# The end of attention by token tiles, with six smaller edits, in a kernel of three transformer blocks on one core

## What is computed

```python
h = _rmsnorm(x, mix_norm[l])
c_q, c_kv, k_pe, hq, hf, hi, hg = jnp.split(h @ w_in[l], splits, axis=-1)
a = _mla(c_q, c_kv, k_pe, positions, ...)      # 4 heads, causal softmax attention
r = _hgrn2(hq, hf, hi, hg, lower[l], hg_out_norm[l])
x = x + jnp.concatenate([a, r], axis=-1) @ w_out[l]
x = x + (_swiglu(...) if l == 0 else _moe(...))

# _mla: q = _rmsnorm(c_q) @ w_q_b, kv = _rmsnorm(c_kv) @ w_kv_b, both with rotary parts
s = jnp.where(key_idx <= q_idx, qn @ kn.T + qp @ kp.T, NEG_BIG)
o = jax.nn.softmax(s, axis=-1) @ v

# _hgrn2
f = lb + (1.0 - lb) * jax.nn.sigmoid(z)
log_f = jnp.log(f)
k = (1.0 - lb) * jax.nn.sigmoid(-z)
# per chunk, b = cumsum(log_f): attn = sum_d q k exp(b_t - b_s), plus a state carried on
o = _rmsnorm(o, out_norm) * jax.nn.silu(g)
```

## Time and profile before

| | |
|---|---|
| median of 3 runs | 1884.51 us (1883.92 to 1885.49) |
| the profiled execution | 1884.52 us, of which the span is 1882.6 us |
| PE busy | 1859.7 us, 99% of the span |
| DVE, ACT, POOL busy | 1520.7, 1240.1, 402.8 us |
| TensorE clock granted (PEclk) | 9, that is 90% or more, in all 40 slices |
| PE's share of the chain that ended last | 90% |

### The profile page before, as it was taken

How to read it: one execution, slowest core, us unless ns; L and a number is a source line. 1 busy time by engine, 2 the same in 40 slices (tenths; PEclk the granted TensorE clock), 3 DMA queues, 4 the chain that set the end, 5 groups by cost and what they waited for, 6 DMA issues and landing times.

```text
span 1882.6 us, 26088 instructions
## 1 busy us (share of the span) xinstructions
PE 1859.7 (99%) x9336; PEld 1563.7 (83%) x9336; DVE 1520.7 (81%) x1650; ACT 1240.1 (66%) x1484; POOL 402.8 (21%) x206
## 2 busy tenths in 40 slices
PE   9999999999999999999999999999999999999997
PEld 7888889888888888878888888888888888888886
DVE  6745357777776887697699999999999999999997
ACT  6654444444754344565588888888888888888876
POOL 6856870002734000371630000000000000000000
PEclk9999999999999999999999999999999999999999
DMA  9534556665444666534699999999999999999994
GB/s 287 169 123 135 179 179 226 223 232 179 132 138 134 218 238 224 163 125 146 221 381 396 391 383 376 388 395 366 388 367 390 395 364 389 366 387 395 371 396 184
DMA packets 251542, 524.20 MB, mean 278 GB/s; under 512 B 9960, under 2 KB 58736, under 8 KB 251328
## 3 DMA queue, kind: packets, MB, share of 16 engines
q1 hardware_dynamic: 243408, 504.00, 74.7%
q10 hardware_dynamic: 5824, 12.06, 1.8%
q0 software_dynamic: 2224, 7.01, 1.2%
HBM read 507.71 MB, written 15.34 MB: 278 GB/s over the span
## 4 chain that ended last, share of the span: by engine, by line
PE 90%; DVE 7%; ACT 1%; issue 1%; DMA 1%; POOL 0%; SPq 0%; DVEq 0%; ACTq 0%
PE bank L740 24%; PE bank L742 24%; PE bank L741 24%; PE bank L1101 6%; PE bank L1104 3%; PE bank L863 1%; PE bank L1368 1%; PE bank L836 1%; DVE arena L1950 1%; DVE arena L2441 1%; DVE arena L1954 1%; PE bank L1182 1%; DMA arena<-in_w_in 1%; DVE arena L2106 1%; PE bank L842 0%
## 5 line engine op out<-in xcount | busy, mean ns | idle before, releaser
L1999 DVE TENSOR_TENSOR w_lo_sb<-arena,w_hi_sb 128x1024 fp32r<-128x1024 f32 x672 | 807.7, 1223 | 74.0 <-ACT w_hi_sb L1522 43.8
L1522 ACT ACTIVATE w_hi_sb<-arena 128x1024 fp32r<-128x1024 f32 x672 | 711.2, 1062 | 168.6 <-PE bank L742 167.9
L740 PE MATMUL bank<-w_hi_sb,left_sb 128*128 128x512 f32 (+1 forms) x1400 | 553.2, 395 | 1.4 <-POOL w_lo_sb L669 1.3
L742 PE MATMUL bank<-w_hi_sb,left_sb 128*128 128x512 f32 (+1 forms) x1400 | 542.2, 387 | 0.0
L741 PE MATMUL bank<-w_lo_sb,left_sb 128*128 128x512 f32 (+1 forms) x1400 | 541.5, 387 | 0.0
L1542 ACT ACTIVATE w_hi_sb<-arena 128x1024 fp32r<-128x1024 f32 (+1 forms) x269 | 278.2, 1051 | 300.8 <-PE bank L742 218.6
L669 POOL TENSOR_TENSOR w_lo_sb<-arena,w_hi_sb 128x1024 fp32r<-128x1024 f32 (+1 forms) x134 | 341.1, 2564 | 536.9 <-ACT w_hi_sb L1542 473.9
L740 PEld LDWEIGHTS bank<-w_hi_sb,left_sb 128*128 128x128 f32 x1400 | 263.1, 188 | 57.9 <-POOL w_lo_sb L669 3.5
L742 PEld LDWEIGHTS bank<-w_hi_sb,left_sb 128*128 128x128 f32 x1400 | 262.9, 188 | 54.9
L741 PEld LDWEIGHTS bank<-w_lo_sb,left_sb 128*128 128x128 f32 x1400 | 263.4, 188 | 50.9 <-issue 0.7
L740 PE MATMUL bank<-w_hi_sb,hid_hi_sb 128*128 128x512 f32 x656 | 257.3, 392 | 0.1
(11 more groups left out here) (365 smaller groups left out, 1676.1 us busy)
## 6 DMA issues: line engine op xcount, KB each, us to landing
arena<-in_moe_w_gate SPq DMA_DIRECT2D x112, 1024.0 KB, 7.6
arena<-in_moe_w_up SPq DMA_DIRECT2D x112, 1024.0 KB, 8.0
arena<-in_moe_w_down SPq DMA_DIRECT2D x112, 1024.0 KB, 7.8
arena<-in_w_in SPq DMA_DIRECT2D x45, 1024.0 KB, 5.1
arena<-in_w_ffn_in SPq DMA_DIRECT2D x22, 1024.0 KB, 5.1
arena<-in_w_out SPq DMA_DIRECT2D x12, 1024.0 KB, 5.0
arena<-in_w_ffn_out SPq DMA_DIRECT2D x11, 1024.0 KB, 4.8
arena<-in_dense_w_gate SPq DMA_DIRECT2D x11, 1024.0 KB, 5.4
```

Source lines behind the costliest of these rows:

```text
L740: pe.matmul(out, still[0], moving[0], start=start, stop=False)
L742: return pe.matmul(out, still[1], moving[0], start=False, stop=stop)
L1522: act.activation(expert_buffer(w_hi_sb, j), expert_piece(j % MOE_SUBS), ACT.Copy) \
L1999: dve.tensor_tensor(expert_buffer(w_lo_sb, j), expert_piece(j % MOE_SUBS), expert_buffer(w_hi_sb, j).bitcast(F32), ALU.subtract) \
```

## The change

It has seven parts.

1. The tail by token tiles. The names ho, mP, mo, mixT of the pair plan become mP0, mo0, mP1, mixA, mo1, mixB; ho gets gemm banks (two more in that plan, after kvb1) and is copied by ACT. PE's tail is made of turn_weights(t), attend(t) and turn_tile(t). The mixture of one tile of tokens is divided, turned and split by itself (own_share, split_tile), and first_mixed multiplies tile 0's four blocks, then tile 1's, where it took two blocks for both tiles; it now covers what two blocks of weights did.
2. hst's matmuls stand behind kvb0, ahead of level(5), and its copy ahead of level_scale(5).
3. level(3) stands behind the second block of hi, not the first.
4. finish_bounds in four steps, in units 3 to 6 of the FFN.
5. In layer 1 log_rest is made first on ACT, and DVE takes it into n_k first; n_k is complete ahead of n_lf.
6. The root for c is a Sqrt on ACT and a reciprocal on DVE, in place of Ln and Exp.
7. mean_c is a step of its own, one level_take earlier. The semaphore head_root is one for both layers, and a wait for level_diff stands ahead of mpT's copies.

```diff
-                 (f"hqT_{layer}", 2), *level[0:4], (f"cT_{layer}", 3), *level[4:6], (f"hst_{layer}", 1),
+                 (f"hqT_{layer}", 2), *level[0:4], (f"cT_{layer}", 3), level[4], (f"hst_{layer}", 1), level[5],
                  (f"mpT_{layer}", 2), level[6], (f"msc0_{layer}", 2),
-                 level[7], (f"msc1_{layer}", 2), (f"ho_{layer}", 2), (f"mP_{layer}", 3), (f"mo_{layer}", 2),
-                 (f"mixT_{layer}", 4),
+                 level[7], (f"msc1_{layer}", 2), (f"mP0_{layer}", 1), (f"mo0_{layer}", 1), (f"mP1_{layer}", 2),
+                 (f"mixA_{layer}", 1), (f"mo1_{layer}", 1), (f"mixB_{layer}", 3),
...
+        if name.startswith("kvb1"):
+            gemm_at[name.replace("kvb1", "ho")], jobs = jobs, jobs + T
...
+            def first_mixed(name, turn_tile):
+
+                layer = int(name[-1])
+                first = span[f"{name}.0.0"][0]
+                hi_left, lo_left = low_left
+                w_hi, w_lo = ([buffer(a, j, 2, 512) for j in (first, first + 1)] for a in (w_hi_sb, w_lo_sb))
+                read = (pair_end[f"mixA_{layer}"], pair_at[f"mixB_{layer}"] + 1)
+                for t in range(T):
+                    job = gemm_at[f"wo0_{layer}"] + t
+                    b, tokens = gemm_bank[job % 4][:, :], slice(t * P, (t + 1) * P)
+                    pe.wait_ge(sem("gemm_read"), job - 3)
+                    pe.wait_ge(sem("mix_hi_ready"), layer * T + t + 1)
+                    for j in range(2):
+                        pe.wait_ge(sem(lo_count[first + j][0]), lo_count[first + j][1])
+                        for k in range(2):
+                            for w in (w_hi[j], w_lo[j]):
+                                pe.matmul(b, hi_left[:, 2 * j + k, tokens], w[:, k, :],
+                                          start=(j == 0 and k == 0 and w is w_hi[0]), stop=False)
+                    if t == 0:
+                        turn_tile(1)
+                    pe.wait_ge(sem("pair_read"), read[t])
+                    for j in range(2):
+                        for k in range(2):
+                            mm = pe.matmul(b, lo_left[:, 2 * j + k, tokens], w_hi[j][:, k, :], start=False, stop=False)
+                        if t == 1:
+                            mm.then_inc(sem("w_used"), 1)
...
-                gemm(f"hi_{l}", between={0: lambda: level(3), 2: turn_c})
+                gemm(f"hi_{l}", between={1: lambda: level(3), 2: turn_c})
...
                     head_gemm(f"kvb{i}_{l}", Q_RANK // P)
                     if i == 0:
+                        pe.wait_ge(sem("n_kt_ready"), l + 1)
+                        b = pair(f"hst_{l}", 0)
+                        for i in range(HG_HEADS):
+                            mm = pe.matmul(b[:, i * P:(i + 1) * P], n_kt[:, i * P:(i + 1) * P], n_v[:, 0, i * P:(i + 1) * P],
+                                           start=True, stop=True)
+                        mm.then_inc(sem("pair_full"), 1)
                         level(5)
-                pe.wait_ge(sem("n_kt_ready"), l + 1)
-                b = pair(f"hst_{l}", 0)
...
+                def turn_weights(t):
+
+                    for i in range(t + 1):
+                        shown = MLA_HEADS // (t + 1)
+                        pe.wait_ge(sem(f"m_exp_{l}"), t * MLA_HEADS + (i + 1) * shown)
...
+                        tr.then_inc(sem("pair_full"), 1)
+
+                def attend(t):
+
+                    b = pair(f"mo{t}_{l}", 0)
+                    for i, head in enumerate(HEAD_AT):
+                        if i % (MLA_HEADS // (t + 1)) == 0:
+                            pe.wait_ge(sem("pair_read"), pair_at[f"mP{t}_{l}"] + i // 2 * t + 1)
...
+                    mm.then_inc(sem("pair_full"), 1)
+
+                def turn_tile(t):
+
+                    pe.wait_ge(sem("pair_read"), pair_end[f"mo{t}_{l}"])
+                    b = pair(f"mix{'AB'[t]}_{l}", 0)
+                    for k in range(KD // 2):
+                        tr = pe.transpose(b[:, k * P:(k + 1) * P], mix[:, t, k * P:(k + 1) * P], mirror[t])
+                    tr.then_inc(sem("pair_full"), 1)
+
+                turn_weights(0)
...
-                    b = pair(f"ho_{l}", t)
+                    job = gemm_at[f"ho_{l}"] + t
+                    pe.wait_ge(sem("gemm_read"), job - 3)
+                    b = gemm_bank[job % 4]
                     for i in range(HG_HEADS):
...
+                    mm.then_inc(sem("ho_full"), 1)
+                attend(0)
+                turn_weights(1)
+                turn_tile(0)
+                attend(1)
...
-                out_gemm(f"wo_{l}", f"mixT_{l}", {(0, 1): {0: lambda: turn_mix(range(2, 4))},
+                out_gemm(f"wo_{l}", f"mixT_{l}", {(0, 0): turn_tile, (0, 1): {0: lambda: turn_mix(range(2, 4))},
...
+                else:
+                    act.activation(log_rest, bound_rest, ACT.Ln, bias=least_rest).then_inc(sem("rest_log"), 1)
                 split_to(span[f"hf_{l}"][1] + BUFFERS + 1)
                 act.wait_ge(sem("z_abs"), l + 1)
                 act.activation(n_tmp[0], n_tmp[0], ACT.Exp, scale=-1.0).then_inc(sem("z_odds"), 1)
...
-                if l == 1:
-                    act.activation(log_rest, bound_rest, ACT.Ln, bias=least_rest).then_inc(sem("rest_log"), 1)
...
-                link(act.activation(head_rinv[:, 8:12], head_ms[:, 8:12], ACT.Ln))
-                act.activation(head_rinv[:, 8:12], head_rinv[:, 8:12], ACT.Exp, scale=-0.5) \
-                    .then_inc(sem("c_rinv"), 1)
+                act.activation(head_rinv[:, 8:12], head_ms[:, 8:12], ACT.Sqrt).then_inc(sem("c_rinv"), 1)
...
+                for t in range(T):
+                    act.wait_ge(sem("ho_full"), l * T + t + 1)
+                    act.activation(n_o[:, t, :], gemm_bank[(gemm_at[f"ho_{l}"] + t) % 4][:, :], ACT.Copy) \
+                        .then_inc(sem("gemm_read"), 1)
+                act.wait_ge(sem("gemm_read"), gemm_at[f"ho_{l}"] + T)
...
-            def finish_bounds():
...
+            def finish_bounds(step):
+
+                if step == 0:
+                    dve.wait_ge(sem("bounds_exp"), 1)
+                    link(dve.tensor_tensor(bound_sum, bound_rest, bound_low, ALU.add))
+                    link(dve.tensor_scalar(least_rest, ident[:, 0:1], 0.0, LEAST_REST, ALU.mult, ALU.add))
+                elif step <= 2:
+                    part = bound_sum[:, (step - 1) * 256:step * 256]
+                    link(dve.reciprocal(part, part))
+                else:
+                    mul(bounds, bounds, over(bound_sum, 1, 2))

             def ffn(tag, norm_tag, done, next_tag):
                 for u in range(FFN_UNITS):
-                    if tag == "f2" and u == 3:
-                        finish_bounds()
+                    if tag == "f2" and 3 <= u < 7:
+                        finish_bounds(u - 3)
...
+                    dve.wait_ge(sem("rest_log"), 1)
+                    link(dve.scalar_tensor_tensor(n_k, n_z, 0.0, over(log_rest, 1, T), ALU.max, ALU.subtract))
                     dve.wait_ge(sem("z_odds"), 2)
                     link(dve.scalar_tensor_tensor(share, n_z, 0.0, odds, ALU.is_ge, ALU.max))
                     mul(share, share, over(bound_rest, 1, T))
                     dve.wait_ge(sem("z_soft"), 2)
                     link(dve.scalar_tensor_tensor(odds, odds, 1.0, over(bound_low, 1, T), ALU.add, ALU.mult))
                     dve.tensor_tensor(odds, odds, share, ALU.add).then_inc(sem("f_ready"), 1)
-                    link(dve.scalar_tensor_tensor(n_k, n_z, 0.0, soft, ALU.max, ALU.add))
+                    dve.tensor_tensor(n_k, n_k, soft, ALU.add).then_inc(sem("n_k_ready"), 1)
                     dve.wait_ge(sem("f_log"), 1)
                     dve.tensor_tensor(n_lf, odds, soft, ALU.subtract).then_inc(sem("n_lf_ready_1"), 1)
-                    dve.wait_ge(sem("rest_log"), 1)
-                    dve.tensor_tensor(n_k, n_k, over(log_rest, 1, T), ALU.subtract).then_inc(sem("n_k_ready"), 1)
+                    dve.wait_ge(sem("n_k_ready"), 2)
...
                 level_diff(4)
                 level_scale(3)
+                mean_c()
                 level_take(2)
                 normalize_c()
                 level_take(3)
...
                 level_take(4)
+                copy_out(f"hst_{l}", 0, n_st)
                 level_scale(5)
                 level_diff(6)
...
                 level_scale(6)
                 level_take(5)
                 level_diff(7)
-                copy_out(f"hst_{l}", 0, n_st)
+                dve.wait_ge(sem(f"level_diff_{l}"), 2 * len(LEVELS))
                 copy_out(f"mpT_{l}", 0, n_pqT[:, :, :].rearrange("p k c -> p (k c)"))
                 copy_out(f"mpT_{l}", 1, n_pkT, width=TOKENS)
...
+                def own_share(t):
+
+                    some = slice(t * MLA_HEADS, (t + 1) * MLA_HEADS)
+                    dve.wait_ge(sem(f"m_exp_{l}"), (t + 1) * MLA_HEADS)
+                    link(dve.reciprocal(row_rec[:, some], row_sum[:, some]))
```

(21 more changed lines are left out.)

99 lines of the change are left out of this document (21 added, 78 removed).

## The result

The changed kernel takes 1893.14 us (median of 6 runs, 1892.67 to 1893.68), beside 1885.15 us (1883.92 to 1886.2) for the kernel before on the same chips: a ratio of 1.0043, with a 95% interval from 1.003 to 1.0056. The forecast was 1887.6 with a range from 1884.0 to 1890.2, so the time lies outside, on the slower side. The profiled run took 1893.59 us with a span of 1890.9, 8.3 more than before.

What follows compares the result with a forecast made beforehand. PE, busy 1859.7 of 1882.6 us, was taken to bound the kernel, so only its idle time could change. The terms: 1884.52 + 7.6 - 3.4 - 1.2 + 0.1 = 1887.6 us, range 1884.0 to 1890.2.

Steps and rivals of the forecast that it cites:

- What bounds the kernel: Whole kernel: PE is busy 1859.7 of 1882.6 us, so the time can only move by what PE stands idle.
- an idle of x us costs about x + 0.16: PE's waits throughout: the last matmul of a run ends 0.16 us after the next could have started.
- Part 1, hst: Both layers, hst moved ahead of level 5: new stalls at level 5 and the scores, +3.8 a layer, +7.6 us.
- the circle isn't closed: Rival, faster: DVE's chain behind hst's copy isn't what the scores (L1232) wait for; 1878.6 us; chance 0.07.
- Part 2, the tail: Tail of both layers, by tiles: PE's waits cost 0.8 in place of 2.4 to 2.5, -1.7 a layer, -3.4 us.
- Part 3, the bounds: FFN: the bounds' quotient spread over four units removes PE's wait of 1.0 for low halves; -1.2 us.
- Part 4, the front: Layer 1's front: a stall of 3.7 at n_lf against a loss of 3.5 that goes, +0.1 us.
- Another hold before level_scale(3): Rival, slower: one more DVE instruction held by POOL in layer 1 makes level(3) wait, +2.1, 1889.7 us; chance 0.17.
- The drain that the Trainium skill puts behind a table load: Rival, slower: a drain of about 1.38 us at each table switch puts +1.4 on n_lf, 1889.0 us; chance 0.03.
- n_lf not pushed: Rival, the same: POOL's subtractions fall as now and layer 1's front gains 3.1, 1884.5 us; chance 0.13.
- Slower: Outcome for the whole kernel: a time more than 0.2% above before; chance 0.39, beside same 0.54 and faster 0.07.

Runs made afterwards that it cites:

- a repeat: The kernel before with one more, useless copy of hst's bank on DVE ahead of mpT's copies in each layer; 1887.11 us.

## Why the prediction was wrong, by its own steps

**What bounds the kernel: right, but for one word.** "The time can only move by what PE stands idle" left out that PE's own pace can move. The step that failed is the next one, "an idle of x us costs about x + 0.16". I had read it off waits of 0.3 to 1.3 us, and used it for waits of about 1.5, 2.9 and 3.3; the longest in the list of before is 1.5, at the very start of the kernel. Up to 1.6 a longer wait costs what it is longer by (0.73 and 0.74 for a repeat). The constant is short too: by the starts of the kernel before, an idle of x costs x + 0.21 to 0.26, since the start behind the first matmul comes late as well; that cancels where a wait only grows. At 2.3 it held in one layer and cost 1.4 more in the other. At 2.7 and 2.9 it cost 1.7 more each time, and at 3.0 2.8. The three waits of the changed kernel make 5.1, against the 4.9 between the forecast change (3.1) and the measured one (8.0); what else was off, a gain of the tail put 0.8 too high and a gain of the front, clock aside, put 0.8 too low, cancels. I listed what the new waits would be and never asked what the clock would do behind them. One place in the trace of the kernel before could have told: PE's last matmul there ends at 1872.8, and the granted clock falls to half 2.5 us later, at 1875.4, while ACT and DVE make the last norm.

```profile
1872.00:1873.00 1.00, 0.84 (x2) 1.00 0.05 16
...
1875.00:1876.00 1.00, 0.00 (x0) 0.69 0.06 16
1876.00:1877.00 1.00, 0.00 (x0) 0.50 0.00 0
```

It costs nothing there, and I took nothing from it. A rival "a wait of about 3 us takes the clock", at some us of half clock behind each, was what was missing.

The Trainium skill, "TensorE: Matmul & The Clock Gate", section "Why this matters for your kernels", warns of idle gaps between bursts of matmuls for this very reason. The traces agree in kind: the clock fell behind the long idle gaps and not behind those of 1.7 us or less. The gap that it names as dangerous is longer, though, than the waits of 2.03 to 2.95 behind which the clock fell here; the measurement decides.

**Part 1, hst.** The mechanism and both waits were right: 1.65 forecast and 1.74 (1.58 and its 0.16) measured at level 5; at the scores 552.47 + 3.8 forecast, and 557.08 less the 0.83 by which the trace was late already, 556.25, measured. The rival in which the circle isn't closed (0.07) is refuted by both rows. Off by 1.5 a layer, for the clock.

**Part 2, the tail.** The mechanism and the idle times were right (0.31 and 0.16). The term was mis-sized by 0.4 a layer: four stops put at 0.8 cost 1.3, by their starts, and the four that they replace, put at 2.4, cost 2.7.

**Part 3, the bounds.** 1.2 forecast, 1.3 measured.

**Part 4, the front.** The count of holds was right: 2.9 and three of 3.4 forecast; 2.83, 3.31, 3.32 and 3.30 measured. n_lf came 17.7 after abs began, 18.3 were forecast. level(3) and turn_c gave 1.7, where 1.5 were forecast. In waits alone the front with level(3) gave 0.7, where I had a loss of 0.1; the clock made a loss of 1.0 of it.

**The rivals.** Another hold before level_scale(3), which had 0.17: no, L1193 doesn't wait there. The drain that the Trainium skill puts behind a table load ("ScalarE: Activation LUTs", "What ACT_TABLE_LOAD costs"): no, ACT's Ln starts 0.01 behind the end of its load (L1752: load at 793.85 for 1.28, ACTIVATE at 795.14). n_lf not pushed: no. Slower had 0.39 and should have had most: the missing rival would have added to every case in which the new waits come.

## What to carry to other kernels

Where TensorE is busy 99% of the time and bounds the kernel, a wait isn't priced by its length alone: here single waits up to 1.7 us left the clock alone, and behind those of 2.0 to 3.0 the engine mostly also ran 3.4 to 6.8 us at half its clock, and that stands in no list of waits. Look at the granted clock in narrow windows behind the longest wait before believing a sum. And when a consumer's copy is moved forward in an in-order list, ask what in that list the producer itself waits for: here that closed a circle, which cost 10.4 us where the copy on the path was worth 1.4.
